# Projection products between the steps of a blocked inverse: six pieces of 12 for twelve of 6

## What is computed

```python
def gdn_chunk(S, q, k, v, g, beta):
    ...
    kk = jnp.einsum('bhtd,bhsd->bhts', k, k)
    L = jnp.where(strict, beta[..., None] * kk * decay, 0.0)
    A = L + jnp.eye(T, dtype=L.dtype)
    ...
    sol = lax.linalg.triangular_solve(A, rhs, left_side=True, lower=True,
                                      unit_diagonal=True)
    ...
```

## Time and profile before

| | us |
|---|---|
| median of 3 runs | 941.87 (940.94 to 942.08) |
| profiled execution | 940.75 |
| its span | 939.0 |
| PE busy | 923.9 |
| DVE busy | 645.8 |
| ACT busy | 440.7 |
| POOL busy | 172.1 |

### The profile page before, as it was taken

One profiled execution on the slowest core, in us unless ns is written; L12 is line 12 of the kernel. 1 busy time (PEld: TensorE's weight loads), 2 busy tenths in 40 slices (PEclk: granted clock), 3 DMA queues, 4 the chain that ended last, 5 costly groups with the idle time before them and its releaser, 6 DMA issues.

```text
span 939.0 us, 16773 instructions
## 1 busy us (share of the span) xinstructions
PE 923.9 (98%) x6897; PEld 838.6 (89%) x6897; DVE 645.8 (69%) x1054; ACT 440.7 (47%) x788; POOL 172.1 (18%) x198
## 2 busy tenths in 40 slices
PE   9999999999799999999999999999999999999998
PEld 8899889999789877799788999999999999888886
DVE  7627888774975565652666999999999999435321
ACT  6634454644675454554654445444444445333310
POOL 0071101102965331000002022222222220000000
PEclk9999999999899999999999999999999999999999
DMA  8624143124204093234904222222222224322221
GB/s 304 222 93 146 49 163 105 46 90 132 81 4 136 1 320 126 91 135 165 323 7 154 106 80 90 91 90 91 90 89 73 73 81 165 135 68 90 82 86 57
DMA packets 75330, 106.34 MB, mean 113 GB/s; under 512 B 2766, under 2 KB 54134, under 8 KB 74870
## 3 DMA queue, kind: packets, MB, share of 16 engines
q1 hardware_dynamic: 75254, 105.27, 33.6%
HBM read 94.89 MB, written 10.37 MB: 112 GB/s over the span
## 4 chain that ended last, share of the span: by engine, by line
PE 55%; DVE 2%; ACT 1%; issue 0%; DVEq 0%; ACTq 0%
PE bank L1230 8%; PE bank L1231 8%; PE bank L1229 8%; PE bank L544 5%; PE bank L543 5%; PE bank L545 5%; PE bank L473 3%; PE bank L491 2%; PE bank L493 2%; PE bank L492 1%; PE bank L569 1%; PE bank L1043 1%; PE bank L571 1%; PE bank L570 1%; PE bank L1045 1%; PE bank L1044 1%
## 5 line engine op out<-in xcount | busy, mean ns | idle before, releaser
L2173 DVE TENSOR_TENSOR wlo<-wraw,whi 128x2048 fp32r<-128x2048 f32 (+1 forms) x56 | 127.2, 2272 | 101.7 <-ACT whi L1636 93.1
L1636 ACT ACTIVATE whi<-wraw 128x2048 fp32r<-128x2048 f32 (+1 forms) x58 | 109.3, 1885 | 100.1 <-PE bank L545 72.9
L505 PE MATMUL bank<-hhi,whi 128*128 128x320 f32 x352 | 115.7, 329 | 6.0 <-DVE wlo L2173 6.0
L507 PE MATMUL bank<-hhi,wlo 128*128 128x320 f32 x352 | 109.1, 310 | 0.0
L506 PE MATMUL bank<-hlo,whi 128*128 128x320 f32 x352 | 109.0, 310 | 0.0
L505 PEld LDWEIGHTS bank<-hhi,whi 128*128 128x128 f32 x352 | 66.5, 189 | 10.1 <-DVE wlo L2173 6.1
L506 PEld LDWEIGHTS bank<-hlo,whi 128*128 128x128 f32 x352 | 66.5, 189 | 1.6 <-issue 1.0
L507 PEld LDWEIGHTS bank<-hhi,wlo 128*128 128x128 f32 x352 | 66.4, 189 | 0.0
L543 PE MATMUL bank<-whi,hhi 128*128 128x512 f32 x150 | 58.4, 389 | 0.0
L544 PE MATMUL bank<-wlo,hhi 128*128 128x512 f32 x150 | 58.4, 389 | 0.0
L545 PE MATMUL bank<-whi,hlo 128*128 128x512 f32 x150 | 58.3, 389 | 0.0
(11 more groups left out here) (493 smaller groups left out, 2660.2 us busy)
## 6 DMA issues: line engine op xcount, KB each, us to landing
wraw<-in_w_in SPq DMA_DIRECT2D x13, 1024.0 KB, 5.3
wraw<-in_w_gate SPq DMA_DIRECT2D x11, 1024.0 KB, 5.2
wraw<-in_w_up SPq DMA_DIRECT2D x11, 1024.0 KB, 5.1
wraw<-in_w_down SPq DMA_DIRECT2D x10, 1024.0 KB, 5.0
kTs<-in_cache_sb_k SPq DMA_DIRECT2D x8, 512.0 KB, 4.5
vraw<-in_cache_sb_v SPq DMA_DIRECT2D x8, 512.0 KB, 5.1
wraw<-in_w_mix_out SPq DMA_DIRECT2D x4, 1024.0 KB, 7.8
kmT<-in_cache_mem_k SPq DMA_DIRECT2D x8, 512.0 KB, 6.3
```

The costliest lines, as they stand in the source:

```text
L505: T.matmul(o, wh[:, k, cs], hhi[:, k, hs], start=(k == 0), stop=False)
L507: ins = T.matmul(o, wl[:, k, cs], hhi[:, k, hs], start=False, stop=(k == KD - 1))
L1636: V(wv(whi, i), wv(wraw, i), ACT.Copy).then_inc(s["w_hi_ready"], 1)
L2173: V.tensor_tensor(wv(wlo, i), wv(wraw, i), wv(whi, i).bitcast(F32), ALU.subtract)\
```

## The change

```diff
-        PIECE_AFTER = range(1, 24, 2)
+        PIECE_AFTER = range(3, 24, 4)
...
             def fill_piece():
                 if not pieces:
                     u = next(fills)
-                    pieces.extend((u, range(k, k + 2)) for k in range(0, KD, 2))
+                    pieces.extend((u, range(k, k + 4)) for k in range(0, KD, 4))
                 u, ks = pieces.pop(0)
                 unit(*u, at="few", ks=ks)
```

## The result

The changed kernel takes 946.69 us (median of 4 runs, 945.72 to 946.86) against 941.48 before (4 runs, 940.94 to 942.08): 1.0058 times, 95% interval 1.0046 to 1.0070, or 5.2 us slower. The forecast was 946.2. The profiled executions are 946.71 and 940.75, their spans 945.0 and 939.0.

A forecast was written before the change was run, and what follows sets the result against it. PE, busy 98% of the span, was taken as the bound. Terms 0.87 + 0.73 + 1.98 + 1.43 = 5.0 us gave 945.8 on the profiled 940.75, 946.9 on the median; forecast 946.2, range 943.4 to 948.6.

The forecast's parts named there:

- (a): Stage start, steps 2 and 3: the first piece no longer covers PE's waits, so step 4 begins later; +0.87 us.
- (b): First four steps in a row, 4 to 7: third and fourth wait for blocks that DVE subtracts and transposes; +0.73 us.
- (c): Four groups behind, steps 8 to 23: ACT's copies alone set the waits, 4.945 us a group; +1.98 us.
- (d): PE's clock at the stage's start: stays at 1.2 GHz through the first piece of 12; +1.43 us.
- PE's second gap: Sign at the stage's start: PE stands a second time, 1.5 to 2 us, before step 3.
- ACT's copies of a group: Sign in the groups: ACT's copies of four steps stand in one unbroken row of 3.1 us.
- a clock that does not care: Rival at the stage's start: the clock ignores the second gap, so only +3.6 us, 944.3; 22%.
- later slack: Rival behind the stage: PE's later waits take up the delay, the end comes to some 943, no difference; 16%.
- waits stay covered: Rival in the groups: no waits, six ways in and out of a piece saved, faster at 939.5; 8%.
- the clock falls inside the groups: Rival in the groups: PE's clock drops on small products with waits between, +7.2 us more, 953; 9%.

The follow-up runs named there:

- busyfirst: Kernel before with only the first piece moved (12 products after step 3), plus 26 and 6 extra products in PE's two gaps: 941.51 us.
- busy6: Kernel before with 24 extra products of ones behind step 1, where PE waits: 941.51 us against 941.69.
- half12: Changed kernel with one of ACT's two copies of each Y left out in levels 1 to 5: 944.12 us, 2.6 us under the changed kernel.
- half6: Kernel before with one of ACT's two copies of each Y left out in levels 1 to 5: 941.27 us against 941.69.
- late12: Kernel before with only the later groups changed: pieces of six after steps 1, 3, 5, 7, pieces of 12 after 11, 15, 19, 23: 943.85 us.
- busy12b: Changed kernel with 26 extra products of ones between steps 1 and 2 and 6 between steps 2 and 3: 944.68 us.
- first12: Kernel before with only the first piece moved: 12 products after step 3, then six after 5, 7, 9 and so on: 943.45 us against 941.53.
- early_six: Kernel before, pieces of six after every second step, with the pieces' block cut early on ACT and DVE: 941.26 us, ratio 0.9998.
- early_twelve: Early cut on ACT and DVE with pieces of 12 after steps 3, 7, 11 and so on: 945.42 us, 4.2 over the same with pieces of six.

## Why the prediction was right

By its own steps, with the 6.0 us of the two timelines divided up:

- *(a)* 0.87 for the first piece's lost cover: 0.90 at step 4 in the timelines of `busyfirst` and `busy6`. Step 2 began at 253.43 (253.34 stated) and step 3 where it had. Carrying it to the end failed in that pair: the times differ by nothing.
- *(b)* 0.73 for the first group: 0.87 (5.20 for 4.33). Its third step came 1.84 us behind the first (1.79 stated), its fourth 2.63 behind (2.5). The second transpose's end had been taken as half of a row of two, 0.38 us; each takes 0.45. This term rests on the timelines alone.
- *(c)* 1.98 for the four groups behind: 2.51 (285.99 - 265.68 = 20.31, for 17.80). The mechanism was right, ACT's copies, and `half12` and `half6` show it. The size was off by one number: I took 0.10 us from the end of a copy to the start of the step, the lag read off DVE. Behind ACT it is 0.25 (267.19 to 267.44) and 0.26 (267.97 to 268.23), which moves the fourth step from 2.38 to 2.55 behind the first, and a group from 4.945 to 5.13.
- *(d)* 1.43 for the clock: the rest of step 4's 2.62 us is 1.7, and the times of the changed kernel with and without the gaps filled differ by 2.0. Step 3 had been left out of the term: it takes 1.07 us (255.91 to 256.98) at the low clock and took 0.80 before.

Of the signs, PE's second gap was 1.36 us and not 1.5 to 2, and ACT's copies of a group stand in two rows with 0.18 us between them and not in one unbroken row, since ACT waits for the third step's product.

The sum 5.0 stood against 6.0 in the two profiled executions and 5.2 in the medians: the profiled execution of the kernel before is one of its quicker ones (940.75; the medians of its runs are 941.4 to 941.7). A part of this is the clock, as the forecast suspected. In the profiles of `late12` and `half6`, whose products stand in the same order up to step 4, it is back later than in the kernel before. There it was 0.79 over 256 to 257, so back at about 256.4; here, of `late12` and then of `half6`:

```profile
257.00:259.00 2.00, 2.00 (x50) 1.81 (x54) 0.87 (x2) 0.80 (x3) 1.92 (x4) 0.83 0.00 0
...
257.00:259.00 2.00, 2.00 (x26) 1.78 (x30) 0.87 (x2) 0.34 (x1) 1.92 (x4) 0.63 0.00 0
```

That is about 257.7 and 258.5, and their step 4 begins 12.5 and 12.9 us after step 0, against 12.0. So the nearness of 5.0 to 5.2 is in part luck. In times, the clock is 2.0 us (`busy12b`), the later groups 2.3 (`late12`) and, from the timelines, the first group 0.9; together 5.2, with nothing left for (a). By that count the three others were taken too small by some 1 us, and (a) filled that up. Each of these differences is uncertain by 0.5 to 1 us, so that (a) comes to nothing in the changed kernel too is likely and not shown.

Of the rivals, the first (a clock that does not care) falls with `busy12b`. The second (later slack) falls with the span: L1043 and L992 wait as long as before, and the stage's 6.0 us are still there at the end. The third (waits stay covered) falls with the groups of 5.13. The fourth (the clock falls inside the groups) falls too: it is 1.00 over 262 to 271 with PE busy 7.89 of 9 us, and over the rest of the stage.

The windows tell when the clock came back: between 256.4 and 258.5 in the three where PE's work behind the first gap was unbroken, between 260 and 261.6 in the five where a second gap broke it (the changed kernel, `first12`, `half12`, `early_six`, `early_twelve`). The Trainium skill's page TensorE: Matmul & The Clock Gate (Part 1) says that the throttled state is the default and activity releases it; the trace agrees, with every return behind broken work later than every return behind unbroken work. The swing that the same page of the Trainium skill tells of under psum-queue depth-cycling did not come in the groups.

## What to carry to other kernels

Work that fills in between dependent steps is worth its place, not its size: grouping it saved some 0.33 us per group in ways in and out (4.34 us before, against the 4.0 that the prediction adds up for a group without waits), and uncovered 1.1 us of waits (5.13 against 4.0). Before small fillers are merged, read how long the copy-back of one step takes and from which engine, with that engine's own lag, and look which long wait the first filler shortens. A gap on TensorE should be filled with work from behind it as long as the place that this work leaves has enough left: 18 products won 2.3 us where they were taken from a cover of 24, and with all of the cover gone more than half of the gain was lost again at the other end.

## What was not expected of the hardware

- A run's time goes in steps with the clock: the version with 24 products behind step 1 took 937 at 1.000 and 940 at 0.996, for the same instructions. A mean of 0.996 is, by an estimate, some 7 us at 0.50 (0.004 x 937 x 2). That is worth up to 3 us there, while the kernel before, at 0.996, gains nothing measurable from 1.000.
- The clock's return moves by 2 us between executions that do the same up to there (256.4, 257.7 and 258.5), and step 4 moves by up to 0.9 us with it. One profile of the kernel before is thus not its typical one.
- PE's stream of small products thins out by 0 to 1.2 us over some 22 us, differently from one execution to the next, with "issue" as its only name. In groups that wait for ACT the starts of the groups do not show it. Its cause is open.
- The profile's releaser was wrong for waits of about 0.6 us, three times in one kernel, because another engine's work ended 0.05 to 0.07 us before the wait did. From the end of the work that counted to the start of the step were 0.25 us behind ACT, and 0.10 behind DVE.
